# One layer of a hybrid encoder: the normalisation of the attention probabilities moves from the vector engine to GpSimd

## The reference, cut to what matters

```
logits = (q . k_sel) * DH_A ** -0.5 - alibi_slopes * dist      # -inf where not valid
p = softmax(logits, axis=-1)
out = p . v_sel                                               # 8 query heads, one K/V head
```

## Time and profile before

| | |
|---|---|
| three runs, us | 2861.80, 2865.97, 2872.58 (median 2865.97) |
| span of the profiled execution, us | 2870.8 (its own device time is not listed apart; the run nearest to it is 2872.58) |
| busy over the span | PE 2711.6 (94%), DVE 1198.2 (42%), ACT 700.1 (24%), POOL 725.5 (25%) |
| attention | about 1577 to 1776 us of the span, 199 us |
| busy within it | PE 179.5, DVE 155.2, ACT 134.9, POOL 37.6 us |
| the multiplications on DVE (L1711 and L1713) | 26.1 and 13.4 us busy, 40 and 12 instructions |

### The profile page before, as it was taken

How to read it: one execution, slowest core, us unless ns; L and a number is a source line. 1 busy time by engine, 2 the same in 40 slices (tenths; PEclk the granted TensorE clock), 3 DMA queues, 4 the chain that set the end, 5 groups by cost and what they waited for, 6 DMA issues and landing times. The chain is left out here.

```text
span 2870.8 us, 39037 instructions
## 1 busy us (share of the span) xinstructions
PE 2711.6 (94%) x15459; PEld 2619.8 (91%) x15459; DVE 1198.2 (42%) x2109; ACT 700.1 (24%) x1258; POOL 725.5 (25%) x396
## 2 busy tenths in 40 slices
PE   7999999999998899999876898998999999999998
PEld 6999999999997599999864686998999999999998
DVE  5121222222234699999544795423222222212126
ACT  5111111111114311211163774212311111111112
POOL 5322222222214012111221311422422222222221
PEclk8999999999999999999966899999999999999999
DMA  4111111111103111132222201431111111111101
GB/s 136 34 45 45 45 44 32 44 45 45 45 1 125 39 46 44 55 93 84 86 45 51 45 1 56 140 114 52 45 45 45 36 39 45 45 45 40 35 30 74
DMA packets 193661, 154.81 MB, mean 54 GB/s; under 512 B 32292, under 2 KB 178128, under 8 KB 193244
## 3 DMA queue, kind: packets, MB, share of 16 engines
q1 hardware_dynamic: 193500, 152.45, 17.9%
HBM read 124.56 MB, written 23.90 MB: 52 GB/s over the span
## 5 line engine op out<-in xcount | busy, mean ns | idle before, releaser
L356 PE MATMUL f1ps_up<-xn_lo,f1w_hi 128*128 128x384 f32 x1056 | 356.6, 338 | 18.5 <-issue 9.7
L356 PE MATMUL f2ps_up<-xn_lo,f2w_hi 128*128 128x384 f32 x1056 | 356.5, 338 | 16.7 <-issue 10.5
L357 PE MATMUL f2ps_up<-xn_hi,f2w_lo 128*128 128x384 f32 x1056 | 355.4, 337 | 0.0
L357 PE MATMUL f1ps_up<-xn_hi,f1w_lo 128*128 128x384 f32 x1056 | 355.3, 336 | 0.0
L358 PE MATMUL f2ps_up<-xn_hi,f2w_hi 128*128 128x384 f32 x1056 | 355.1, 336 | 0.0
L358 PE MATMUL f1ps_up<-xn_hi,f1w_hi 128*128 128x384 f32 x1056 | 355.0, 336 | 0.0
L356 PE MATMUL d_ps<-xn_lo,d_w_hi 128*128 128x384 f32 x888 | 302.0, 340 | 7.0 <-POOL xn_lo L311 5.5
L357 PE MATMUL d_ps<-xn_hi,d_w_lo 128*128 128x384 f32 x888 | 300.7, 339 | 0.0
L358 PE MATMUL d_ps<-xn_hi,d_w_hi 128*128 128x384 f32 x888 | 300.6, 339 | 0.0
L508 DVE TENSOR_TENSOR f2hid<-f2gate,f2ps_up 128x384 f32<-128x384 f32 x66 | 36.6, 554 | 519.1 <-ACT f2gate L477 519.1
L508 DVE TENSOR_TENSOR f1hid<-f1gate,f1ps_up 128x384 f32<-128x384 f32 x66 | 36.6, 554 | 518.4 <-ACT f1gate L477 518.4
(11 more groups left out here) (302 smaller groups left out, 5397.7 us busy)
## 6 DMA issues: line engine op xcount, KB each, us to landing
f1raw<-in_w_ffn_up SPq DMA_DIRECT2D x44, 512.0 KB
f2raw<-in_w_ffn_up SPq DMA_DIRECT2D x44, 512.0 KB
d_raw<-in_w_in SPq DMA_DIRECT2D x37, 512.0 KB, 4.1
p_dram<-stage SPq DMA_DIRECT2D x21, 576.0 KB, 3.1
f1raw<-in_w_ffn_down SPq DMA_DIRECT2D x11, 1024.0 KB
f2raw<-in_w_ffn_down SPq DMA_DIRECT2D x11, 1024.0 KB
b_sg<-p_dram SPq DMA_DIRECT2D x16, 576.0 KB, 4.9
x_dram<-xT SPq DMA_DIRECT2D x1, 4608.0 KB, 15.0
```

Of the source, the lines that this page charges most:

```text
L356: nc.tensor.matmul(out, w_hi, x_lo, start=first, stop=False)
L357: nc.tensor.matmul(out, w_lo, x_hi, start=False, stop=False)
```

## The change

`normalise` moves into GpSimd's program as one `tensor_scalar` for each head, and DVE keeps the reciprocal, now called `inverse`. GpSimd waits for `inv_ok`, and its last instruction of an item signals `pn_ok`, for which PE's transposes wait as before. The reciprocal of item i waits for `pn_ok` of item i - 2, whose buffer of `t_inv` it takes. `normalise(i + 1)` stands in GpSimd's program ahead of the low parts of iteration i; `query_lo` gets one more wait.

```diff
             @block.gpsimd
             def _(pool):
-                def query_lo(t, m):
+                def query_lo(t, m, n):
                     pool.wait_ge(qh_ok, 2 * (t + 1))
+                    if n:
+                        pool.wait_ge(pn_ok, n)
...
+                def normalise(i, split):
+                    t, _, g = ITEMS[i]
+                    pool.wait_ge(ql_ok, 2 * (split + 1))
+                    pool.wait_ge(inv_ok, i + 1)
+                    for y in range(g):
+                        p = heads(pr, i)[:, y]
+                        last = nc.gpsimd.tensor_scalar(p, p, inv[:, i % 2, y:y + 1], None, ALU.mult)
+                    last.then_inc(pn_ok, 1)
...
+                normalise(0, split)
                 for i, (t, x, g) in enumerate(ITEMS):
+                    if i + 1 < len(ITEMS):
+                        normalise(i + 1, split)
                     if t + 2 < NTP and i + 1 == FIRST[t + 1]:
                         split = t + 2
-                        query_lo(split, m)
+                        query_lo(split, m, min(i + 2, len(ITEMS)))
...
-                def normalise(i):
+                def inverse(i):
                     t, _, g = ITEMS[i]
                     dve.wait_ge(p_ok, i + 1)
+                    if i >= 2:
+                        dve.wait_ge(pn_ok, i - 1)
                     v.reciprocal(inv[:, i % 2, 0:g], sm[:, i % 2, 0:g]).then_inc(inv_ok, 1)
-                    dve.wait_ge(inv_ok, i + 1)
-                    if g == 1:
-                        p = pr[:, i % 2, 0:keys(t)]
-                        v.tensor_scalar(p, p, inv[:, i % 2, 0:1], None, ALU.mult).then_inc(pn_ok, 1)
-                    else:
-                        v.tensor_tensor(heads(pr, i), heads(pr, i),
-                                        inv[:, i % 2, 0:g, None].to_broadcast([P, g, keys(t)]), ALU.mult)\
-                            .then_inc(pn_ok, 1)
```

More of the change, by code:

```diff
@@ L1591, in output_lo @@
                                             ALU.subtract).then_inc(lo, 1)
-                query_lo(0, 0)
-                query_lo(1, 0)
+                def normalise(i, split):
[6 more added lines that the diff above has]
+                    last.then_inc(pn_ok, 1)
+                query_lo(0, 0, 0)
+                query_lo(1, 0, 0)
                 m, split = 0, 1
+                normalise(0, split)
                 for i, (t, x, g) in enumerate(ITEMS):
+                    if i + 1 < len(ITEMS):
+                        normalise(i + 1, split)
                     if t + 2 < NTP and i + 1 == FIRST[t + 1]:
                         split = t + 2
-                        query_lo(split, m)
+                        query_lo(split, m, min(i + 2, len(ITEMS)))
                     if i >= LAST[m] + 2:
@@ L1721, in _ @@
                 for i, (t, x, g) in enumerate(ITEMS):
-                    normalise(i)
+                    inverse(i)
                     if i + 2 < len(ITEMS):
```

## The result

The changed kernel takes 2923.54 us (median of four runs, 2912.07 to 2927.78). The kernel before, run beside it, took 2867.66 (four runs, 2861.80 to 2872.58). The ratio is 1.0179, 95% interval 1.0154 to 1.0204: slower, by 56 us (whether by 2% or a little less, the interval leaves open). The forecast was 2900 with a range of 2864 to 2926. The direction and the place were right, and the growth was 1.6 times the 34 us forecast: inside the range, but outside the forecast's own 2891 to 2906. In what follows, two executions far above all others of their kernel (3104 us with the copy, 9722 us with one instruction for each head on DVE) are left out of the medians and ratios.

A forecast was written before the change was run, and what follows sets the result against it. PE and DVE, both near their limit, wait for each other in a circle over two items. Terms of 25.5 + 0.5 + 0.6 + 3.4 + 3.3 + 0.4 = 33.7 us gave 2900 us, range 2864 to 2926.

The forecast's parts named there:

- circle of two items: In attention, DVE's and PE's waits for each other span two items, so a longer multiplication adds half its growth per item.
- T: GpSimd's multiplication time for one head, claimed as 2.66 ns a column without fixed part: 2.72 us at 1024 columns.
- Rival 2: GpSimd's multiplication in attention runs at the bare 4.40 us row, 3.82 ns a column: 58 us more, 2924 us; chance 0.07.
- rival 1: GpSimd multiplies in attention as fast as it copies, 0.86 ns a column: sum 0, 2866 us, not slower; chance 0.27.
- The hand-over: From reciprocal to GpSimd and from GpSimd to PE, 0.06 us each; with the reciprocal's 0.15, 0.27 us beside the multiplication.
- terms of t = 4 to 7: Key blocks 4 to 7, eight items each: 0.59, 0.73, 0.87 and 1.00 us more an item, 25.5 us in all.
- Rival 3: PE's clock falls in idle time at t = 4 to 7, adding some 21 us to the 34: 2921 us; chance 0.08.
- The end: Last item of attention, with little work beside its multiplication: about 0.6 us more.
- t = 2: Key block 2: DVE's lost work pays for the longer multiplication, 3.70 us an item against 3.68: nothing added.
- The opening: Start of attention: low queries of t = 2 come 1.7 us later, items 0, 1 and 3 add 1.6; together 3.3 us.
- t = 3: Key block 3, four items of two heads: step from 4.04 to 4.89 us, 3.4 us more in all.
- t = 8: Key block 8, PE-bound: multiplication 0.12 us late, half of it an item, 0.5 us for eight items.

## Why the prediction was right, and where it was short

- *The mechanism.* Right. The multiplication sits in a circle of two items, its duration counts half there, and DVE's freed time turns into waiting (102.3 against 18.4 us). Five values of T (0.75 on DVE; 1.04, 1.89, 2.85 and 5.69 on POOL) bear it out, the last only with the clock's part added.
- *T.* 2.72 us forecast for 1024 columns, 2.85 measured. The reading of the earlier trace rows, that POOL had waited for DVE for the first 1.33 of its 4.40 us, fits: 3.07 for 1152 columns, where the fitted line gives 3.16. Rival 2 took the 4.40 as it stood and was wrong. That its sum of 2924 fell on the measured time is luck, and so in part is that the range, which ends just above that sum, holds it: the missing 22 us are of another kind. The Trainium skill's rule of mutual exclusion ("SBUF — State Buffer", section "Who interferes with whom") agrees with these rows, and with the new multiplications, which never stretched beside the logits.
- *The rule of rival 1.* The Trainium skill says ("GPSIMD Engine Reference", section "Engine selection") that one-input elementwise work runs roughly at line rate. The copy took 1.04 us at 1024 columns. The `tensor_scalar`, one-input as well, took 2.85 us, and 2.77 even with an immediate, so for it the rule doesn't hold here, and the measurement decides. The row of the same operation, a single one, in another phase and disturbed, was worth more than the rule.
- *The hand-over.* 0.27 forecast, 0.37 measured: 0.16 from the reciprocal to POOL, 0.05 from POOL to PE, 0.16 the reciprocal itself. The first was taken from the hand-over DVE to PE. T and the hand-over together make the terms of t = 4 to 7 29.5 us in place of 25.5.
- *The clock.* The main size that was off: a term that the sum put at nothing. Rival 3 stood beside the forecast as another case with a chance of 0.08 and some 21 us, and it is a part of what happened: 11 us at t = 5 to 7. My argument against it, one stretch with PE half busy at a clock of 1.00, was weak: one stretch does not show what many in a row do. I also spoke of about 1 us of waiting an item. The mean is right, 51.1 us over 52 items; but the items pair up, and PE stands still for 2.4 to 2.6 us ahead of every second group of transposes. With that pattern three profiled executions had the clock at 0.88 to 0.91 at t = 6; at t = 7 one of the three kept 1.00.
- *The end.* 0.6 forecast, 4.4 measured. In the changed kernel the last items fell to the lower clock; the values of the last item but one in its trace, and in that of the version with the queries first:

```profile
1814.12 1.57 PEld L1675 LDWEIGHTS t_ps_o<-t_pt,vc 128*64 128x64 f32 x8 [0.42 <-issue]
```
```profile
1817.90 0.85 PEld L1678 LDWEIGHTS t_ps_o<-t_pt,vc 128*64 128x64 f32 x8 [0.22 <-issue]
```

  From the last reciprocal to the end it took 11.11 us in the first, at a granted clock of 0.69, and 8.21 in the second, at 1.00, against 6.76 before:

```profile
1809.80:1820.92 11.12, 8.69 (x40) 6.28 (x40) 0.16 (x1) 2.66 (x7) 3.31 (x4) 0.69 0.01 1
1814.57:1822.79 8.22, 5.66 (x40) 4.05 (x40) 0.16 (x1) 2.66 (x7) 3.30 (x4) 1.00 0.01 2
```

  So 1.5 us are the longer T at the end, which I sized too small, and 2.9 the clock.
- *t = 2.* Nothing forecast, 3.0 us measured. The step that failed is "the rest in proportion to the columns", 5.09 us. From the rows it is 2P - D = 2 x 4.57 - (2 x 1.24 + 0.37) = 6.3, and in the versions with the two-input operation and with the copy 2 x 4.14 - (2 x 0.83 + 0.37) = 6.3 and 2 x 3.87 - (2 x 0.51 + 0.37) = 6.4. A likely reason, not tested: that rest holds fixed parts of instructions and hand-overs, which don't shrink with the columns.
- *The opening and t = 3.* 3.3 and 3.4 forecast, 5.3 and 4.5 measured. T without a fixed part made the narrow instructions too short: 0.34 us forecast for 128 columns, 0.60 measured. At t = 3 the step itself was close, 4.89 forecast and 5.02 measured, but partly by luck. The two multiplications took 3.13 us, not 2.72, while the rest was 6.2, not 6.78 (from the two-input version, 2 x 4.32 - (2 x 1.04 + 0.37), and the same from the copy). That makes 4.84 at full clock; 0.7 us of the four items are then the clock, granted 0.93. And the forecast counted from a step of 4.04 where the reciprocals have 3.88. In t = 0 and 1 the clock was lower too (0.55 and 0.67 against 0.70 and 0.85); what that cost was not separated. The wait for the queries of t = 2 grew by 2.1 us, as said (some 2):

```profile
1583.93 3.63 POOL L1601 TENSOR_SCALAR t_p<-t_p,t_inv 128x256 f32<-128x256 f32 x4 [3.21 <-DVE t_inv L1723]
...
1590.44 0.66 PE L1639 MATMUL t_ps_l<-t_k_hi,t_qs 128*128 128x384 f32 x1 [7.11 <-POOL t_qs L1586]
```

  It was 5.00.
- *t = 8.* 0.5 forecast, 1.5 measured. T was 1.605 in place of 1.40 and the hand-over 0.10 longer, which by the rule of half the lateness gives 0.15 an item more, 1.2 us for eight: 1.7 in all.

In sum, of the 26 us by which attention outgrew the forecast (59.7 against 33.7), some 14 are the clock (11 and 2.9), 4 the terms of t = 4 to 7, 3 t = 2, and 5 the opening with `query_lo`, t = 3 (0.7 of it the clock again), t = 8 and the end.

*Still open:* what decides whether the clock falls. The same stretch of the same code was granted 0.92 in one execution and 1.00 in another. At t = 3 all five profiled versions with one `tensor_scalar` for each head on POOL ran under full clock (0.93, 0.93, 0.84, 0.82 and 0.78, the 0.82 under the new order of PE), and the copy and the two-input form at 1.00; why by so different amounts was not traced.

## What to carry to other kernels

Before an operation is moved to an idle engine, find the circle of waits that it sits in: its new duration counts there, whatever the old engine's relief, and freed time on an engine off the bound turns into waiting. Price it by a row of the same instruction, with a fixed part, and take off what another engine's lock put into that row. Where a wait opens on TensorE, ask in which pieces it comes, not only how long it is on the mean, since the clock can add to it (here some 14 of attention's 60 us); and look first whether TensorE's own order can put work into the gap (here the product one item earlier gave back half of the loss, and made the kernel before 0.2% faster).

## What the runs showed of the hardware that was not expected

- On POOL, fp32, 128 x 1024, in place: copy 1.04 us; `tensor_tensor` with the second operand broadcast along the row 1.89; `tensor_scalar` with an immediate 2.77, with an operand in memory 2.85. A two-input operation with two full inputs takes 2.36. So the same product is a third cheaper written as a two-input operation, and `tensor_scalar` is the slowest of these forms.
- `tensor_scalar` on POOL takes 0.28 us + 2.50 ns a column at all nine widths from 128 to 1024.
- Filling PE's gaps with work that nobody needs made t = 5 to 7 shorter, 109.6 against 118.4 us, with the clock at 1.00 throughout, in the one execution profiled.
